# The next expert's upper down half is issued behind all four gate/up pages of the expert two places on

## What is computed

```python
logits = xt @ w_router + b_router            # 256 tokens, 32 experts
top_v, top_i = lax.top_k(logits, 4)
gates = softmax(top_v)
# for each expert e, on the tokens that chose it:
gu = xblk @ w_gate_up[e] + b_gate_up[e]      # 1024 -> 2048
x_glu = minimum(gu[:, :1024], 7); x_lin = clip(gu[:, 1024:], -7, 7)
act = x_glu * sigmoid(1.702 * x_glu) * (x_lin + 1)
y = act @ w_down[e] + b_down[e]              # 1024 -> 1024
# out[token] += gate * y; then an RMS norm, a gain and the residual
```

## Time and profile before

| what | value |
| --- | --- |
| median of 3 runs | 1259.45 us |
| the profiled execution's own time | 1259.95 us |
| its span | 1257.8 us |
| mean granted TensorE clock | 0.934 |
| PE busy | 1036.7 us, 82% of the span |
| DVE busy | 293.4 us, 23% |
| ACT busy | 183.7 us, 15% |
| moved by DMA | 464.61 MB, mean 369 GB/s |
| DMA rate in a saturated slice | 417 to 419 GB/s |

### The profile page before, as it was taken

One profiled execution on the slowest core, in us unless ns is written; L12 is line 12 of the kernel. 1 busy time (PEld: TensorE's weight loads), 2 busy tenths in 40 slices (PEclk: granted clock), 3 DMA queues, 4 the chain that ended last, 5 costly groups with the idle time before them and its releaser, 6 DMA issues.

```text
span 1257.8 us, 21204 instructions
## 1 busy us (share of the span) xinstructions
PE 1036.7 (82%) x8263; PEld 495.3 (39%) x8264; DVE 293.4 (23%) x779; ACT 183.7 (15%) x453; POOL 20.3 (2%) x46
## 2 busy tenths in 40 slices
PE   2799999965965999978988897899699969696965
PEld 1565788642432334323432343343334323232322
DVE  6647422242111111212111212111211211111112
ACT  0211353120110111101100110111011101010012
POOL 1000100100000000000000000000000000000000
PEclk9799999977998999989998999899999989898988
DMA  9979812965999969999999999999999999999995
GB/s 353 379 283 399 302 70 86 387 254 216 417 417 419 418 275 380 419 418 396 414 417 417 374 417 417 417 391 419 418 417 386 419 418 417 418 417 418 417 418 240
DMA packets 92207, 464.61 MB, mean 369 GB/s; under 512 B 5166, under 2 KB 6998, under 8 KB 59292
## 3 DMA queue, kind: packets, MB, share of 16 engines
q1 hardware_dynamic: 91452, 461.71, 91.0%
q0 software_dynamic: 736, 2.63, 0.6%
HBM read 462.22 MB, written 2.11 MB: 369 GB/s over the span
## 4 chain that ended last, share of the span: by engine, by line
PE 47%; DMA 40%; DVE 6%; issue 3%; DVEq 2%; ACT 1%; POOL 0%; SPq 0%; ACTq 0%; POOLq 0%
DMA arena<-in_w_down_dram 36%; PE pp L1268 13%; PE pp L1296 12%; PE pp L1106 4%; DMA arena<-in_w_ada_dram 4%; PE po L1225 3%; PE pp L1038 2%; PE pp L1119 2%; PE po L1175 2%; PE pp L1238 2%; PE pp L1257 2%; DVE arena L714 2%; DVEq L937 2%; PE pp L1276 1%; DVE work L928 1%
## 5 line engine op out<-in xcount | busy, mean ns | idle before, releaser
L1268 PE MATMUL pp<-arena,work 128*32 128x256 f32 (+1 forms) x3840 | 362.3, 432 | 13.3 <-DMA arena<-in_w_gate_up_dram 13.3
L1296 PE MATMUL pp<-arena,work 128*32 128x256 f32 (+1 forms) x1920 | 215.9, 483 | 124.6 <-DMA arena<-in_w_down_dram 94.1
L1268 PEld LDWEIGHTS pp<-arena,work 128*32 128x32 f32 (+1 forms) x3840 | 156.3, 117 | 216.7 <-issue 142.4
L1296 PEld LDWEIGHTS pp<-arena,work 128*32 128x32 f32 (+1 forms) x1920 | 78.9, 127 | 223.1 <-DMA arena<-in_w_down_dram 114.6
L907 DVE TENSOR_SCALAR work<-pp 128x128 f32<-128x128 f32 (+1 forms) x74 | 25.3, 342 | 451.8 <-PE pp L1268 451.8
L636 ACT ACTIVATE work<-work 128x128 f32<-128x128 f32 (+1 forms) x74 | 25.9, 350 | 405.0 <-DVE work L907 405.0
L1238 PE MATMUL pp<-h_sb,work 128*32 128x256 f32 (+1 forms) x480 | 53.6, 453 | 32.2 <-issue 21.1
L1225 PE MATMUL po<-work 64*128 64x512 f32 x304 | 78.3, 635 | 1.6 <-ACT work L650 1.6
L901 DVE COPY work<-pp 128x256 f32<-128x256 f32 (+1 forms) x37 | 19.5, 526 | 235.4 <-PE pp L1238 235.4
L1106 PE MATMUL pp<-arena 128*128 128x256 f32 x256 | 57.4, 382 | 0.0
L714 DVE SCALAR_TENSOR_TENSOR arena<-arena,small 128x1024 f32<-128x1024 f32 x42 | 54.0, 1285 | 8.6 <-DMA arena<-in_w_ada_dram 7.1
(11 more groups left out here) (204 smaller groups left out, 634.1 us busy)
## 6 DMA issues: line engine op xcount, KB each, us to landing
arena<-in_w_gate_up_dram SPq DMA_DIRECT2D x128, 2048.0 KB, 25.6
arena<-in_w_down_dram SPq DMA_DIRECT2D x64, 2048.0 KB, 25.4
arena<-in_w_ada_dram SPq DMA_DIRECT2D x12, 2048.0 KB, 12.6
arena<-in_w_in_dram SPq DMA_DIRECT2D x5, 2048.0 KB, 15.7
arena<-in_w_gate_dram SPq DMA_DIRECT2D x4, 2048.0 KB, 14.5
arena<-in_w_out_dram SPq DMA_DIRECT2D x2, 2048.0 KB, 9.9
arena<-in_w_branch_a_dram SPq DMA_DIRECT2D x1, 2048.0 KB, 18.7
arena<-in_w_branch_b_dram SPq DMA_DIRECT2D x1, 2048.0 KB, 17.5
```

The source lines that it names most:

```text
L1268: mm = t_.matmul(pp[j * m:(j + 1) * m, UP[hh], 0:w].rearrange("p (s f) -> p s f", s=2), hgT[:, at:at + m], gu_w[slot][:, k, :, col:col + w ...
L1296: mm = t_.matmul(pp[j * m:(j + 1) * m, UP[0], 0:w], actT[:, at:at + m], wd[:, j * w:(j + 1) * w], start=(n == 0), stop=(n == KD - 1))
```

## The change

In step n of SP's loop, gate/up pages 1 to 3 of place n + 2 are issued together with page 0, ahead of the wait for `s_y` and of the upper down half of place n + 1. No load and no wait is added or taken away.

```diff
                     load_bgu(slot, e)
-                    load_gu(slot, e, 0)
+                    for q in range(4):
+                        load_gu(slot, e, q)
                     sp.wait_ge(s_y, total)
                     load_dhi(last_e)
                     sp.reg_mov(dhi_expert, e)
-                    for q in range(1, 4):
-                        load_gu(slot, e, q)
                     load_dlo(slot, e)
                     count_blocks(i * 2 + (1 + slot))
```

## The result

The changed kernel takes 1335.96 us (median of 4 runs, 1335.57 to 1336.43) beside 1259.42 us for the kernel before: the ratio is 1.0608, 95% interval 1.0589 to 1.0626. That is 76.5 us slower, where 80.1 were forecast. The profiled execution took 1335.57 us.

A forecast was written before the change was run, and what follows sets the result against it. The expert stage was taken as bound by a stream of 192 weight pages, lengthened whenever it runs dry and by what follows its last page. 60.2 + 12.3 + 7.6 = 80.1 us gave 1339.6 us, range 1326 to 1357.

The forecast's parts named there:

- The mechanism: Weight stream: upper halves land three pages, 15.05 us, later, so fewer pages cover the wait until a two-block expert's next issue.
- Places 9 to 21: Two-block experts at places 9, 13, 17, 21: +15.05 us each, 60.2 us in all; gap 1.4 before, 16.5 after.
- the restart cost that I could not explain: Two-block experts in the old order: 1.3 us of the measured 2.7 us gap beyond the 1.4 worked out.
- The low end of the forecast: Whole kernel: 12.4 us at each of four two-block experts, +66.8 us in all, so 1326 us.
- Place 5: Two-block expert with two wide blocks: +12.3 us, three pages' 15.05 less a 2.8 us gap that goes.
- the second gap: Place 5, old order: 2.8 us between page 0 and the later-issued upper half, gone with four pages at once.
- The tail: End of the kernel, places 30 and 31: last upper halves come later, +7.6 us, up to 9.9 allowed.
- the start: First loads of SP's loop, place 1's upper half four pages after the first: 0, priced at 0 to 2 us.
- One-block experts: Steps of experts with one block: 0 us, next pages issued in time by 5.3 us.
- Queue order: Rival on the load queue: order not kept, upper half lands as early as now, 1256.6 us; chance 3%.
- Slack: Rival on PE's waits: late page hidden behind the stream's slack except at the end, 1267.1 us; chance 3%.
- The clock: Rival at the five two-block experts: low clock reaches the wide block's opening, 5.4 us each, 1366 us; chance 8%.

The follow-up runs named there:

- k = 1: The kernel before: one gate/up page stands ahead of the upper down half in each step; 1259.42 us.
- k = 2: Two gate/up pages ahead of the upper down half in every step, against one in the kernel before; 1278.1 us, ratio 1.014.
- k = 4: The changed kernel: all four gate/up pages ahead of the upper down half in each step, against one before; 1335.96 us, ratio 1.0608.
- one-block kernels: Second blocks left out for every expert, all weights still loaded, against the kernel before; 1239.38 us in the old order, 1246.82 in the new.
- written-out loop: The kernel before with SP's loop written out in 30 steps, order of issues unchanged; 1261.91 us, ratio 1.0014.
- k = 0: No gate/up page ahead of the upper down half; each step waits for down first, against the kernel before; 1274.69 us, ratio 1.011.

## Why the prediction was right

- **The mechanism** held in each step. The upper halves land in the order of issue, at 5.02 us a page; the time from a two-block expert's landing to the next issue is unchanged at 18.8 us; three fewer pages cover it. PE waits for no gate/up page any more (0.0 us in the page's group of L1267, 13.3 before in that of L1268).
- **Places 9 to 21: 55.9 us, forecast 60.2.** 548.57 less 492.67 us, 14.0 each instead of 15.05. This is the step that was mis-sized. The working had a gap of 1.4 now and 16.5 after; measured are 2.7 and 137.14 - 120.43 = 16.7. So the new gap was right to 0.2 us, and the restart cost that I could not explain belongs to the old order and went with it. The low end of the forecast had allowed for that, at 12.4 each. The step from k = 1 to k = 2 shows the same, 4.0 us against 4.98 for each later page. Most of that microsecond is in the stream: the bytes missing in a cycle, as the mean of four, are 2.4 us at k = 1, 6.7 at k = 2 and 16.7 at k = 4, so they grow by 4.3 for the first page and by 5.0 for each later one. In all four cycles at k = 1 the rate sags a second time, 25 to 30 us behind the landing, by 0.4 to 0.9 us in all; at k = 2 there is none of that size at that point. It comes where the single page has run out and the upper half follows, which was issued 3.9 us after it (591.64 and 595.55). Windows of the kernel before, behind place 9:

```profile
598.00:599.00 1.00, 1.00 (x6) 0.39 (x4) 0.18 (x1) 0.00 (x0) 0.00 (x0) 1.00 0.85 315
599.00:600.00 1.00, 1.00 (x8) 0.42 (x4) 0.00 (x0) 0.00 (x0) 0.00 (x0) 1.00 1.04 381
```

That this late second issue is the cause is argued and not tested, and the rest stays open. The size is not sharp either: in the written-out loop with k = 1 the same four cycles take 490.94 us, 122.74 each, which makes the first page 4.5.
- **Place 5: +12.1 us, forecast 12.3.** From 454.63 to 600.30 it is 145.67 us, against 133.53 from 439.32 to 572.85; all four pages go out at 482.05 and the second gap is gone.
- **The tail: +7.0 us, forecast 7.6.** The landings are three pages late from the start: place 5's comes at 454.63 - 439.32 = 15.3 us later (15.05 in the forecast, which had 0 to 2 for the start), and the end is 8.3 us closer behind the last one (22.15 against 30.41). The two one-block kernels put it at 7.4.
- **One-block experts: 0.6 us, forecast 0.** From place 25 to 30 it is 151.21 us against 150.57, within the wobble of the stream given above. The one-block kernels bound all 30 steps by the same 7.4 us.
- The sum is 15.3 + 12.1 + 55.9 + 0.6 - 8.3 = 75.6, and the spans differ by 75.7; the medians differ by 76.5. No two large errors cancel in it.
- **The rivals.** Queue order: refuted by the landings. Slack: 7.4 us is right for one-block experts, and the two-block ones cost the other 69. The clock: it did drop further (0.904 over the span against 0.934), but not into the wide block ahead of the decisive issue, and from the landing to that issue it is 18.8 us as before, so it cost nothing here. It does cost 1.6 to 2.9 us a time in the kernel with the new order in five steps only, where the wait falls into that block itself.
- **What the working lacked.** It tied the loss to the pages behind the two-block expert's own half. The kernel with that half put back (+65 us) shows that this is not the whole condition: it is the pages behind the last landing for which PE really waited. With the same order in each step the two are the same, so the number came out right.

## What to carry to other kernels

In a stream of loads in one queue, moving a load that is free to go early ahead of one that is needed next delays the latter by whole transfer times. That is free as long as the consumer waits for the stream anyway, and costs nearly its full length (14.0 of 15.05 us here) where the stream is about to run dry because the consumer holds the buffers. Look for the longest consumer item, count the transfers queued behind the landing that it waited for, and compare them with the time to its release. If a lag must be taken, take it far enough ahead of that item for an item with slack to make it up. Moving the needed load still further ahead is no remedy by itself: it delays the loads behind it, as the kernel with k = 0 shows.

## What the runs showed that was not expected

- A lag split into two waits (10.68 and 1.33 us) cost no time where it mattered; in one piece (15.87 us) it made the work behind it 1.6 to 2.9 us longer, at a granted clock of 0.71 in that stretch.
- An order changed in 5 of 30 steps cost more (84.6 us) than in all 30 (76.5 us).
- A restart with a single page costs up to 1 us more than one with two or four in a row (4.0 us from k = 1 to 2, or 4.5 in the written-out loop, against 4.98 a page from 2 to 4).
